# A mixed transformer block on one Trainium2 core: other PSUM banks for the recurrence's second key products and two transposes, and VectorE's preparation of the later pair moved into the inverse

## The reference

```python
def step(S, inp):                      # one token, per head; S is 64 x 64
    r_t, w_t, k_t, v_t, a_t, b_t = inp
    sa = jnp.einsum('bhvk,bhk->bhv', S, a_t)
    S = (S * w_t[:, :, None, :] + sa[..., None] * b_t[:, :, None, :]
         + v_t[..., None] * k_t[:, :, None, :])
    return S, jnp.einsum('bhvk,bhk->bhv', S, r_t)
```

## Time and profile before

| what | value |
|---|---|
| median of three runs | 1251.21 us (1249.71 to 1251.71) |
| the profiled execution, its own time | 1245.89 us |
| its span, first to last instruction | 1243.8 us |
| mean granted TensorE clock | 0.968 |
| TensorE matmul busy | 1124.5 us (90%) |
| VectorE busy | 648.4 us (52%) |
| ScalarE busy | 458.1 us (37%) |
| POOL busy | 9.9 us (1%) |
| the six pairs of the recurrence | 471.24 to about 845 us of the span |

### The profile page before, as it was taken

One profiled execution on the slowest core, in us unless ns is written; L12 is line 12 of the kernel. 1 busy time (PEld: TensorE's weight loads), 2 busy tenths in 40 slices (PEclk: granted clock), 3 DMA queues, 4 the chain that ended last, 5 costly groups with the idle time before them and its releaser, 6 DMA issues.

```text
span 1243.8 us, 21886 instructions
## 1 busy us (share of the span) xinstructions
PE 1124.5 (90%) x9476; PEld 837.2 (67%) x9476; DVE 648.4 (52%) x1057; ACT 458.1 (37%) x736; POOL 9.9 (1%) x12
## 2 busy tenths in 40 slices
PE   6999999677799787888888898899799999999998
PEld 4377776344468566666666665668588888888887
DVE  2478777886544666464655643674633323233332
ACT  3233353346642453323232322352445311345211
POOL 0000000000000000000000000000000000000000
PEclk9999999799899898989899999999899999999999
DMA  8832223200022211101010003103233333323330
GB/s 320 294 121 66 85 85 114 73 1 1 1 71 82 74 62 38 38 32 36 19 36 19 19 3 121 52 26 101 61 92 94 102 102 88 99 85 102 102 110 26
DMA packets 25582, 94.93 MB, mean 76 GB/s; under 512 B 2833, under 2 KB 2833, under 8 KB 24977
## 3 DMA queue, kind: packets, MB, share of 16 engines
q1 hardware_dynamic: 25488, 93.54, 23.3%
HBM read 89.34 MB, written 4.19 MB: 75 GB/s over the span
## 4 chain that ended last, share of the span: by engine, by line
PE 50%; DVE 9%; ACT 2%; issue 2%; ACTq 0%; DVEq 0%
PE psum L689 13%; PE psum L690 13%; PE psum L691 13%; PE psum L699 3%; PE psum L987 2%; PE psum L1000 1%; PE psum L1036 1%; DVE pair_weights_low L1663 1%; DVE work L2052 1%; PE psum L955 1%; PE psum L1003 1%; PE psum L1079 1%; DVE work L2014 1%; PE psum L1059 1%; PE psum L1013 1%
## 5 line engine op out<-in xcount | busy, mean ns | idle before, releaser
L1663 DVE TENSOR_TENSOR weights_low<-ring,weights_high 128x1024 fp32r<-128x1024 f32 x72 | 88.2, 1225 | 82.8 <-ACT weights_high L1334 82.8
L1334 ACT ACTIVATE weights_high<-ring 128x1024 fp32r<-128x1024 f32 x72 | 75.9, 1054 | 127.7 <-PE psum L691 127.7
L689 PE MATMUL psum<-normed_high,weights_high 128*128 128x512 f32 x256 | 102.7, 401 | 4.8 <-DVE normed_low L1668 4.2
L690 PE MATMUL psum<-normed_low,weights_high 128*128 128x512 f32 x256 | 102.1, 399 | 0.0
L691 PE MATMUL psum<-normed_high,weights_low 128*128 128x512 f32 x256 | 101.9, 398 | 0.0
L689 PE MATMUL psum<-hidden_high,weights_high 128*128 128x512 f32 x256 | 99.6, 389 | 0.0
L690 PE MATMUL psum<-hidden_low,weights_high 128*128 128x512 f32 x256 | 99.6, 389 | 0.0
L691 PE MATMUL psum<-hidden_high,weights_low 128*128 128x512 f32 x256 | 99.6, 389 | 0.0
L1284 ACT ACTIVATE work<-psum 128x384 f32<-128x384 f32 (+2 forms) x124 | 59.6, 510 | 96.1 <-PE psum L1036 51.0
L689 PE MATMUL psum<-pair_normed_high,pair_weights_high 128*128 128x512 f32 x176 | 76.6, 435 | 12.3 <-DVE normed_low L1668 4.3
L2141 DVE TENSOR_TENSOR hidden_low<-work,hidden_high 128x512 fp32r<-128x512 f32 x32 | 22.2, 693 | 110.3 <-ACT hidden_high L1573 110.3
(11 more groups left out here) (235 smaller groups left out, 2115.2 us busy)
## 6 DMA issues: line engine op xcount, KB each, us to landing
ring<-weights SPq DMA_DIRECT2D x154, 512.0 KB, 3.6
residual<-xT SPq DMA_DIRECT2D x1, 2048.0 KB, 18.4
residual_saved<-residual SPq DMA_DIRECT2D x8, 256.0 KB, 2.0
residual<-residual_saved SPq DMA_DIRECT2D x1, 2048.0 KB, 8.7
outT<-residual SPq DMA_DIRECT2D x8, 256.0 KB, 3.2
work<-memT SPq DMA_DIRECT2D x1, 1024.0 KB, 5.0
work<-ctxT SPq DMA_DIRECT2D x1, 1024.0 KB, 9.7
small_sb<-small SPq DMA_DIRECT2D x1, 907.0 KB, 7.7
```

The lines of the kernel that those rows point to most:

```text
L689: pe.matmul(out, wh, high(k), start=first and n == 0, stop=False)
L690: pe.matmul(out, wh, low(k), start=False, stop=False)
L1334: act.activation(WH[group(q)][:, q % 2, :], ring[:, SLOT[b], :], ACT.Copy).then_inc(w_high, 1)
L1663: vec.tensor_tensor(WL[group(q)][:, q % 2, :], ring[:, SLOT[b], :], WH[group(q)][:, q % 2, :].bitcast(F32), ALU.subtract).then_inc(w_low, 1)
```

## The change

The banks: ka goes to 6 and 7, tk to 4 and tv to 5. VectorE: MAK and MRK move from the head into the level b = 4 (b = 2 in the last pair), `changed_key`, `decayed_r` and the weight subtraction "r" for the later pair move from the end of the pair before into the level b = 4 of pairs 1 to 4, behind `decayed_a`, and the weight subtraction "v" moves from the level b = 8 behind all levels. `least_norm` stays where it was. ScalarE: the two instructions of the reciprocal norm become `key_norm`, and for pairs 2 to 5 they run behind the four copies out of PSUM. The instructions themselves and their number are the same.

```diff
@@ -228,8 +228,8 @@
         final = p == NP - 1
         if final:
             side_banks[0] = (4, 5, 6)
-        o.extend([(f"nf_{p}", 2, 0), (f"na_{p}", 2, 2), (f"ka_{p}", 2, 4)])
-        o.extend((f"{x}_{p}", 1, n) for n, x in enumerate(("ta", "tb", "tk", "tv")))
+        o.extend([(f"nf_{p}", 2, 0), (f"na_{p}", 2, 2), (f"ka_{p}", 2, 6)])
+        o.extend((f"{x}_{p}", 1, n) for n, x in zip((0, 1, 4, 5), ("ta", "tb", "tk", "tv")))
         for n, b in enumerate(LEVELS):
             first = n % 2 * 2
             o.extend((f"y{b}_{p}_{h}", 1, first + h) for h in range(HEADS))
@@ -1478,6 +1478,8 @@
                 act.activation(HS[:, 0, :], K0, ACT.Square, scale=col("k_k", p)).then_inc(kk_sq, 1)
                 shift_start(f"r_{p}", MU_PAIR + 3 * p + 1, R0)
 
+            def key_norm(p):
+
                 act.wait_ge(*is_free(f"kks_{p}"))
                 link(act.activation(HR[:, 0, :], HR[:, 0, :], ACT.Ln, scale=KK_SCALE))
                 act.activation(HR[:, 0, :], HR[:, 0, :], ACT.Exp, scale=-0.5,
@@ -1498,13 +1500,17 @@
                 rms(f"gv_{p}", HR[:, 1, :], S, 1.0 / DH, GN_EPS, gn_rs)
 
             pair_inputs(0)
+            key_norm(0)
             pair_values(0)
             pair_inputs(1)
+            key_norm(1)
             for p in range(NP):
                 if p:
                     act.wait_ge(*is_full(f"yu_{p - 1}"))
                 for x, out in (("ta", TAM[:, :, :, 0:C]), ("tb", TM[:, :, :, 0:C]), ("tk", TK), ("tv", TV)):
                     copy_out(f"{x}_{p}", out, src=bank(f"{x}_{p}").rearrange("p (c h t) -> p c h t", c=G, h=HEADS))
+                if p and p + 1 < NP:
+                    key_norm(p + 1)
                 for b in LEVELS:
                     if b == LEVELS[3]:
                         copy_out(f"mv_{p}", TAM[:, :, :, C:2 * C],
@@ -2015,10 +2021,7 @@
                 free_inc(vec.tensor_tensor(TM[:, :, :, C:2 * C].rearrange("p c h t -> p h c t"),
                                            by_head(f"na_{p}")[:, :, :, 1], mask("upto", HEADS, G), ALU.mult),
                          f"na_{p}")
-                vec.wait_ge(*is_full(f"ka_{p}"))
-                vec.tensor_tensor(MAK, by_head(f"ka_{p}")[:, :, :, 0], mask("before", HEADS, G), ALU.mult)
-                free_inc(vec.tensor_tensor(MRK, by_head(f"ka_{p}")[:, :, :, 1], mask("upto", HEADS, G), ALU.mult),
-                         f"ka_{p}")
+                late = p + 1 if p and p + 1 < NP else None
                 for b in LEVELS:
                     for h in range(HEADS):
                         name = f"y{b}_{p}_{h}"
@@ -2028,10 +2031,19 @@
 
                     if p and b == LEVELS[0]:
                         gn_centre(p - 1)
+                    if b == LEVELS[0 if p == NP - 1 else 1]:
+                        vec.wait_ge(*is_full(f"ka_{p}"))
+                        vec.tensor_tensor(MAK, by_head(f"ka_{p}")[:, :, :, 0], mask("before", HEADS, G), ALU.mult)
+                        free_inc(vec.tensor_tensor(MRK, by_head(f"ka_{p}")[:, :, :, 1], mask("upto", HEADS, G),
+                                                   ALU.mult), f"ka_{p}")
                     if p == NP - 1:
                         memory_unit(2 * LEVELS.index(b))
                     if p + 1 < NP and b == LEVELS[1]:
                         decayed_a(p + 1)
+                        if late:
+                            changed_key(late)
+                            decayed_r(late)
+                            weights_after(late, "r")
                     if p + 1 < NP and b == LEVELS[2]:
                         pair_input(p + 1, "v")
                     if p + 1 < NP and b == LEVELS[3]:
@@ -2058,8 +2070,6 @@
                         memory_unit(2 * LEVELS.index(b) + 1)
 
                     if p + 1 < NP:
-                        if b == LEVELS[2]:
-                            weights_after(p + 1, "v")
                         if b == LEVELS[0]:
                             unit_key(p + 1)
                         if b == LEVELS[3]:
@@ -2067,6 +2077,8 @@
                 def by_pair(x):
                     return x.rearrange("p (c q) t -> p q c t", q=PARITIES)
 
+                if p + 1 < NP:
+                    weights_after(p + 1, "v")
                 vec.wait_ge(*is_full(f"gr_{p}"))
                 gr = by_parity(f"gr_{p}").rearrange("p q (c n) -> p q c n", c=G)
                 vec.tensor_tensor(by_pair(GT), gr[:, :, :, 0:C], mask("eye", PARITIES, G), ALU.add).then_inc(gt_ready, 1)
@@ -2102,11 +2114,7 @@
                 vec.wait_ge(*is_full(f"yh_{p}"))
                 free_inc(vec.tensor_tensor(CAT[:, p, :], bank(f"yh_{p}"), CAT[:, p, :], ALU.add), f"yh_{p}")
                 if p + 2 < NP:
-                    weights_after(p + 2, "r")
-                if p + 2 < NP:
-                    changed_key(p + 2)
                     least_norm(p + 2)
-                    decayed_r(p + 2)
                 elif p + 1 < NP:
                     memory_queries(1)
             memory_unit(MU_CHAIN + len(CHAIN))
```

## The result

The changed kernel takes 1218.34 us (median of four runs, 1216.83 to 1223.20) against 1251.46 for the kernel before: a ratio of 0.9736, with a 95% interval of 0.9704 to 0.9768, or 33 us less. The profiled execution took 1216.83 us.

What follows compares the result with a forecast made beforehand. TensorE was taken as the bound, busy 1124.5 of 1243.8 us, with holes and a lowered clock in the heads. Savings 27.0 + 3.3 + 1.3 + 0.2 = 31.8 us, from median 1251.21 to 1219.4 us; range 1213.5 to 1230.

Steps and rivals of the forecast that it cites:

- VectorE before the masks: Heads of pairs 1 to 4: only least_norm stays ahead, so pair 1's first mask starts 4.47 us earlier.
- The head's sum: Pairs 1 to 4, nf to y4: head of 8.86 us after the change, gains together 27.0 us.
- The clock stays up: Heads of pairs 1 to 4: granted clock at 1.00, as in pair 5's head despite its 1.37 us hole.
- rival A: Heads of pairs 1 to 4: holes go but the clock still falls; saving 18.2 us, time 1233; chance 0.09.
- Level b = 4: Second level, pairs 1 to 4: 6.3 us of moved VectorE work hidden behind TensorE's projections, 0.4 us to spare; cost zero.
- Rival B: VectorE overflows the second level, y8 starts 0.9 us late in four pairs; saving 28 us, time 1223; chance 0.12.
- Rival C: Level b = 4: VectorE's queue before the x4 additions becomes the path; at 9.7 us per pair 1258 us, slower; chance 0.02.
- The subtraction of v: Moved from before the y16 masks to behind the levels: 0.8 us in pairs 1 to 4, 0.1 in pair 0, together 3.3.
- Pairs 0 and 5: Holes of 1.36 and 1.37 us before tk and tv go: 1.3 us gained in pair 0, 0.2 in pair 5.
- The range: Whole kernel: 1213.5 to 1230 us; the upper end takes in rival B and two thirds of the way to rival A.

Runs made afterwards that it cites:

- order experiment: Changed kernel with the old banks for ka, tk and tv and with MAK and MRK back in the head; 1224.80 us, ratio 0.9801.
- The filled hole: Kernel before, with 18 useless 128-column matmuls in TensorE's hole between na and ka of pairs 1 to 4; 1246.32 us, ratio 0.9965.

## Why the prediction was right

**The total.** 1219.4 us was forecast and 1218.3 measured; the saving was 31.8 against 33 by the runs and 32.4 in the recurrence by the traces. The single terms were less exact than their sum. The terms that were foreseen came out 3.5 us larger than forecast, and 2.9 us were lost in places that the forecast didn't have; that the two nearly cancel is luck.

**VectorE before the masks: right.** The first mask came 1.37 us after nf, as worked out (1.38). The order experiment shows that this is the step that counts: with the old banks the heads of pairs 1 to 4 already won 23.5 of their 29.2 us.

**The head's sum: right in mechanism, short by 2.2 us.** 27.0 us were forecast, 29.2 measured. The step "nf to y2 5.32 us" came to 4.77: durations of single rows were added for ka and the transposes (1.08, 1.09, 1.09), but rows that follow each other overlap, and the distances are what adds up (64 key products in 1.89, from 527.45 to 529.34, and 16 transposes in 1.89). The division of pair 1's 6.08 us into 3.6 for the holes and 2.5 for the slow ka and transposes does not hold as a price list: with the hole filled and the clock up, pair 1 gained 0.72 us. Either part is worth that much only once VectorE is early. And y2 to y4 was at the upper clock before only in pairs 1 and 3; in pairs 2 and 4 it took 4.25 and 5.37 us instead of 3.54. The gains were taken from whole heads, so the sum has this in it.

**The clock stays up: right**, and rival A fell: 1.00 in all four heads. The filled hole shows the link directly: VectorE as late as before, no long hole, no lower clock. The forecast rested on pair 5's hole of 1.37 us; no head of the changed kernel's pairs 1 to 4 has such a hole, and the order experiment kept 1.00 with one of 1.21. Elsewhere the clock did fall behind holes of that size in some traces (see the last section). By the Trainium skill (TensorE: Matmul & The Clock Gate, Part 4: PE-mode transpose) transposes don't count as busy for the clock gate in the way that other matmuls do; 16 of them in a row would then be a gap of 1.9 us, and the trace shows no lower clock behind them in any head.

**Level b = 4: right.** It took in the moved work and had 0.62 us left before the second addition (0.4 was forecast). Its inner course was another: POOL's product did not hold the COPY but came too late for that. It ran 1.77 us instead of 1.27, beside decayed_r at first, and the weight subtraction took 2.33 us instead of 1.22: it ended 1.07 us after POOL did. The forecast had one wait for POOL in it, at the COPY; there was one, at the subtraction, so the sum held although the place was wrong. The sum of COPY, decayed_r and subtraction was 2.94 us, 3.14 was forecast. Rival B did not happen, but one more instruction of 0.7 us begins to show it. Rival C needed 7.9 us per pair; five more instructions made the level 3.5 us longer.

**The subtraction of v: right.** 0.83 us in each of pairs 1 to 4 and 0.16 in pair 0, 3.5 in all where 3.3 were forecast.

**Pairs 0 and 5: low.** 1.58 and 0.94 us in the heads, where 1.3 and 0.2 were forecast. In both the bank of tk and tv brings 1.6 us to y2. In pair 5 the two masks take back 0.64 of it, the difference to the run with them in the head, and not their whole 1.2.

**What the sum left out.** The terms as measured make 35.3 us, the recurrence became 32.4 shorter. Two things took the rest back: the chain of pair 4 (19.09 instead of 17.57 us, the clock fell behind the old hole of 2.19 us) and a stop of 1.46 us in level b = 8 of pair 3, which made that level 1.3 us longer. The hole of pair 4's chain in the kernel before, the stretch behind it, and the stretch in the changed kernel from 1 us behind its hole:

```profile
759.62 0.50 PE L689 MATMUL psum<-pair_normed_high,pair_weights_high 128*128 128x512 f32 x1 [2.19 <-DVE work L1589]
...
759.62:764.60 4.98, 4.98 (x33) 3.60 (x34) 0.57 (x2) 0.00 (x0) 0.00 (x0) 1.00 0.01 3
...
730.94:734.89 3.95, 3.95 (x17) 2.67 (x16) 0.28 (x1) 0.00 (x0) 0.00 (x0) 0.57 0.01 4
```

This loss belongs to the kernel before as well: with only the banks changed the chain took 20.31 us. Twelve of the fourteen traces have the hole, and the profiled execution of the kernel before is the only one of them in which the clock stayed up behind it. The second loss is not explained by any wait:

```profile
652.17 0.27 PE L1003 MATMUL psum<-work 64*64 64x64 f32 x1 [1.46 <-issue]
```

It is no accident of one execution. The stop stands at the same place, with 1.18 to 1.72 us, in both traces of the changed kernel and in six of its variants; with MAK and MRK in the head it is 0.64 us, and it is in neither the kernel before nor its two variants, nor in the kernel with the order alone, nor with five more instructions in the level ahead of it. What makes TensorE stop there stays open; it was not tried.

**The range.** Its lower end, added from its own terms, is about 1214 us rather than 1213.5, and two thirds of the way to rival A is 1228.5 rather than 1230. Neither bears on the outcome.

## What to carry to other kernels

Look at what stands in an engine's own queue ahead of the instruction that the others wait for: here six instructions that nobody needed for another 10 us (a weight subtraction, changed_key's three, decayed_r's two) held back the banks of kks, nf and na and with them the start of the inverse. A hole on TensorE has two prices, its length and the slow matmuls behind it; the second can be measured by filling the hole with useless matmuls. And a bank change without the order behind it only moves the wait: look for the next releaser before counting the first wait as won.

## What the runs showed of the hardware

- Holes on TensorE of 1.20 to 1.47 us left the granted clock at 1.00 in every head of the order experiment. Behind 2.60 to 2.65 us in the heads of the kernel before it fell each time, in pairs 1 and 3 at once, in pairs 2 and 4 only during or after ka. Behind 2.19 us in pair 4's chain it fell in eleven of twelve traces. Matmuls without use (4.29 us of them) kept it up.
- A hole of 1.3 us did not always leave the clock up. In the last pair's levels two holes of 1.40 and 1.31 us stand 5 to 6.4 us apart in every trace. In ten of the fourteen the clock stayed up behind both; in four it fell, and y16 to the last update then took 13.1 to 13.6 us instead of 11.8. The order experiment, the row behind the second hole and the two stretches of 2 us from there:

```profile
777.03 0.67 PE L699 MATMUL psum<-memory_keys_values,work 64*128 64x256 f32 x2 [1.31 <-DVE mixed L1984]
...
777.03:779.03 2.00, 2.00 (x22) 1.33 (x24) 1.00 (x4) 0.65 (x3) 0.00 (x0) 1.00 0.00 0
779.03:781.03 2.00, 2.00 (x26) 1.43 (x22) 0.85 (x2) 0.19 (x1) 0.00 (x0) 0.52 0.00 0
```

- POOL's product and VectorE's instructions between SBUF tiles held each other up as whole instructions: beside each other the subtraction took 2.33 us and POOL's product 1.77, apart 1.22 and 1.27. In these traces the one that started first was not held up: before, POOL was first and the COPY took 0.86 us, ending with POOL's product; after, the COPY was first and took 0.17. The Trainium skill (SBUF — State Buffer, SBUF: two separate sides) describes an exclusive lock on the port pair that the two engines share, held for a whole instruction by whichever starts first. Both traces agree with it: the subtraction ended 1.07 us after POOL's product, within 0.15 us of its own 1.22.
- The recurrence began between 469.94 and 476.93 us in the profiles of these kernels, although the program ahead of it was the same in all. One profile each is therefore no measure of a gain below some 5 us in the whole span; the heads of pairs 1 to 4 agreed to 0.02 us between kernels that share them. Not every stage did: level b = 4 of pair 4 took 8.97 to 9.37 us in traces of kernels that don't differ there.
